# The second feed-forward matrix as a seven-product block scheme, interleaved with tiles of the first

## The reference, cut to what matters

```
f = rms_norm(h, g_ffn_pre)                    # [256, 2048]
f = square(relu(f @ w_ff1)) @ w_ff2           # w_ff1 [2048, 8192], w_ff2 [8192, 2048]
h = h + rms_norm(f, g_ffn_post)
```

## Time and profile before

| | |
|---|---|
| median of 3 runs | 2152.32 us (2152.02 to 2153.08) |
| span of the profiled execution | 2150.6 us |
| PE busy | 2125.1 us (99%) |
| DVE busy | 1361.9 us (63%) |
| ACT busy | 1106.1 us (51%) |
| POOL busy | 156.2 us (7%) |
| DMA, mean | 184 GB/s |
| PE clock granted, mean | 0.999 |

### The profile page before, as it was taken

The page is one execution under the profiler, slowest core; times in us unless marked ns, Lnnn a source line. Parts: engine busy times, 40 slices in busy tenths (PEclk is TensorE's granted clock), DMA queues, the critical chain, the costliest instruction groups (busy, mean ns, idle before and its releaser), DMA issues. The chain is left out here.

```text
span 2150.6 us, 29240 instructions
## 1 busy us (share of the span) xinstructions
PE 2125.1 (99%) x11602; PEld 1841.8 (86%) x11602; DVE 1361.9 (63%) x1979; ACT 1106.1 (51%) x1541; POOL 156.2 (7%) x78
## 2 busy tenths in 40 slices
PE   8999999999999999999999999999999999999998
PEld 7888888888988888888888888888888888888886
DVE  5554568875577558876578678766555555555555
ACT  4444554454464555555455455656435534544543
POOL 0000000000000000000007873000000000000000
PEclk9999999999999999999999999999999999999999
DMA  8666545655576655655656654646666666666664
GB/s 278 196 189 187 165 138 174 179 172 186 185 214 186 178 148 159 174 167 176 191 180 198 193 178 151 215 136 206 193 193 190 189 193 193 189 194 190 192 190 145
DMA packets 325031, 395.17 MB, mean 184 GB/s; under 512 B 20848, under 2 KB 252912, under 8 KB 324128
## 3 DMA queue, kind: packets, MB, share of 16 engines
q1 hardware_dynamic: 323104, 383.21, 59.0%
q0 software_dynamic: 1792, 10.10, 1.2%
HBM read 391.16 MB, written 2.10 MB: 183 GB/s over the span
## 5 line engine op out<-in xcount | busy, mean ns | idle before, releaser
L490 DVE TENSOR_TENSOR low<-raw,high 128x1024 fp32r<-128x1024 f32 (+2 forms) x672 | 809.9, 1209 | 639.0 <-ACT high L934 635.3
L934 ACT ACTIVATE high<-raw 128x1024 fp32r<-128x1024 f32 (+2 forms) x732 | 763.0, 1046 | 775.8 <-PE acc L682 201.7
L682 PE MATMUL acc<-xhl,high 128*128 128x512 f32 x3198 | 766.4, 391 | 0.0
L682 PEld LDWEIGHTS acc<-xhl,high 128*128 128x128 f32 x3198 | 587.0, 188 | 113.8 <-issue 0.7
L699 PE MATMUL acc<-xhl,low 128*128 128x256 f32 x3200 | 436.9, 286 | 1.9 <-DVE xhl L1792 1.4
L699 PEld LDWEIGHTS acc<-xhl,low 128*128 128x128 f32 x3200 | 414.4, 191 | 18.1 <-DVE xhl L1792 1.8
L686 PE MATMUL acc<-high,yhl 128*128 128x512 f32 (+1 forms) x1036 | 380.1, 373 | 2.2 <-DVE work L1718 1.6
L687 PE MATMUL acc<-high,yhl 128*128 128x512 f32 (+1 forms) x1036 | 378.8, 372 | 0.0
L702 PE MATMUL acc<-low,yhl 128*128 128x512 f32 (+1 forms) x1036 | 241.9, 374 | 0.2
L686 PEld LDWEIGHTS acc<-high,yhl 128*128 128x128 f32 x1036 | 195.2, 188 | 36.8 <-DVE work L1718 2.0
L687 PEld LDWEIGHTS acc<-high,yhl 128*128 128x128 f32 x1036 | 195.2, 188 | 33.8
(11 more groups left out here) (228 smaller groups left out, 1286.9 us busy)
## 6 DMA issues: line engine op xcount, KB each, us to landing
raw<-in_w_in SPq DMA_DIRECT2D x328, 512.0 KB, 3.7
raw<-in_w_ff SPq DMA_DIRECT2D x256, 512.0 KB, 3.9
raw<-in_w_out SPq DMA_DIRECT2D x91, 512.0 KB, 4.3
raw<-in_w_mem_kv SPq DMA_DIRECT2D x32, 512.0 KB, 5.0
raw<-in_w_in SPq DMA_DIRECT2D x16, 256.0 KB, 2.7
raw<-in_w_out SPq DMA_DIRECT2D x10, 256.0 KB, 2.8
x_nat<-in_mem SPq DMA_DIRECT2D x4, 512.0 KB, 7.8
x_nat<-in_x POOLq DMA_DIRECT2D x4, 512.0 KB, 6.4
```

The lines of the kernel that those rows point to most:

```text
L490: eng.tensor_tensor(part(low, g), part(raw, g), part(high, g).bitcast(F32), ALU.subtract).then_inc(ready, 1)
L682: ins = pe.matmul(acc[:, 2 * (c.acc % 2) + s, :], wh[:, t, at], vhl, start=first, stop=last)
L934: act.activation(part(high, g), part(raw, g), ACT.Copy).then_inc(high_ready, 1)
```

## The change

In mathematics: for the first 28 of 32 pairs of 128-row hidden tiles, and for half of the columns in the last 4 pairs, the 2x2 block product (two halves of the 256 rows, a pair of 128-row tiles, two halves of 1024 columns) is computed with seven block products in place of eight. A *group* is one such product: 256 hidden rows by 1024 columns of `w_ff2`, 60 groups in all. What is left of the matrix (4 pairs, columns 1024 to 2047) is done in 8 blocks as before (`last_block`).

- PE alternates: `group(g)`, 21 matmuls of 512 columns (seven products, for each the terms high-high, low-high, high-low one behind the other, each product in its own PSUM bank), and `hidden_tile(g+6)`, one tile of 128 hidden columns (16 matmuls of 512 columns, 16 of 256). The seven banks are emptied every fourth group.
- SP loads a group as two 512 KB transfers into one of two buffers (`load_group`), once PE has used the group two before.
- POOL forms the sums of the weight blocks (`group_sums`: two subtractions of 512 elements per partition, one of 1024), the sums of the hidden blocks (`pair_sums`: four of 128 elements, every second group) and the last additions (`add_sums`: two of 1024 elements, every fourth group).
- ACT rounds the seven weight units in three parts (`split_h`), the seven hidden units (`pair_h`), and copies a tile out of PSUM.
- DVE takes the low parts (`split_l`: 1024, 1024 and 1536 elements; `pair_l`: 896 every second group), folds and squares a hidden tile (`hidden_rows`: two of 256), takes the low parts of the two blocks of `w_ff1` (L518, in place in `raw`), and empties the banks (`sums_out`: seven of 512 every fourth group).

The core of the diff:

```diff
+PRODUCTS = ((2, 2, 1), (3, 3, 6), (1, 0, 0), (5, 1, 3), (6, 4, 4), (7, 5, 5), (4, 6, 2))
 PE
+            def group(g):
+                pe.wait_ge(pair_ready, pair + 1)
+                hid, units = hidden(pair), bset_r[:, g % 2]
+                for n, (p, unit, combo_no) in enumerate(PRODUCTS):
+                    pe.wait_ge(split_high, 3 * g + (1, 1, 2, 2, 3, 3, 3)[n])
+                    if first:
+                        product_released(g // 4, p)
+                    for hl in range(2):
+                        pe.matmul(bank_of[p], hid[:, hl, combo_no, :], units[:, 7 + unit, :], start=first and hl == 0,
+                                  stop=False)
+                    pe.wait_ge(split_low, 3 * g + (1, 1, 2, 2, 3, 3, 3)[n])
+                    ins = pe.matmul(bank_of[p], hid[:, 0, combo_no, :], units[:, unit, :], start=False, stop=last)
+                ins.then_inc(group_used, 1)
+            for g in range(GROUPS):
+                group(g)
+                if g + TILES_AHEAD < TILES:
+                    hidden_tile(g + TILES_AHEAD)
+            for i in range(4):
+                last_block(2, i, (0, 1))
 ACT
+            for g in range(GROUPS):
+                n, ahead = g + TILES_AHEAD - 1, g + 1 < GROUPS
+                if g and n < TILES:
+                    tile_copy(n)
+                if ahead:
+                    split_h(g + 1, 0)
+                    split_h(g + 1, 1)
...
+                round_block(FF1 + 2 * g + 2)
...
+                if ahead:
+                    split_h(g + 1, 2)
+                if g % 2 == 0 and n < TILES:
+                    pair_h(g // 2 + 2)
+                round_block(FF1 + 2 * g + 3)
 DVE
+            def split_l(g, part_no):
+                dve.wait_ge(sum_step, 3 * g + 3)
+                dve.wait_ge(split_high, 3 * g + part_no + 1)
+                at, end = ((2, 4), (0, 2), (4, 7))[part_no]
+                dve.tensor_tensor(bset_r[:, g % 2, at:end, :], bset[:, g % 2, at:end, :], bset_r[:, g % 2, 7 + at:7 + end, :].bitcast(F32),
+                                  ALU.subtract).then_inc(split_low, 1)
+            for g in range(GROUPS):
...
+                if g and n < TILES:
+                    hidden_rows(n)
+                if g:
+                    low_block(FF1 + 2 * g)
+                    low_block(FF1 + 2 * g + 1)
+                if ahead:
+                    split_l(g + 1, 0)
+                    split_l(g + 1, 1)
+                if g % 4 == 3:
+                    sums_out(g // 4)
+                if ahead:
+                    split_l(g + 1, 2)
+                if g % 2 == 0 and n < TILES:
+                    pair_l(g // 2 + 2)
 SP
+            def load_group(g):
+                if g < 2:
+                    sp.wait_ge(xt_ready, 40)
+                else:
+                    sp.wait_ge(group_used, g - 1)
...
 POOL
+            def group_sums(g):
+                units = bset[:, g % 2]
+                pool.wait_ge(group_landed[g % 2][0], 16 * (g // 2 + 1))
+                pool.tensor_tensor(units[:, 1, :], units[:, 1, :], units[:, 0, :], ALU.subtract).then_inc(sum_step, 1)
...
+            for g in range(GROUPS):
+                if g + 1 < GROUPS:
+                    group_sums(g + 1)
+                if g % 2 == 0 and g + TILES_AHEAD - 1 < TILES:
+                    pair_sums(g // 2 + 2)
+                if g % 4 == 0 and g:
+                    add_sums(g // 4 - 1)
```

More of the change, by code:

```diff
@@ L653, in weight_block @@
                 wh, wl = part(high, g), part(low, g)
-                tiles = [(t, c.kt0 + c.nk * i + t, s) for t in range(c.nk) for s in rows[:len(outs)]]
+                tiles = [(t, c.kt0 + c.nk * i + t, s) for t in range(c.nk) for s in range(2)]
                 crossed = k == ("f1", 0, 0) and i == 0
@@ new lines, in product_released @@
+            def product_released(k, p):
+                if k == 0:
+                    if p in (5, 6, 7, 4):
+                        pe.wait_ge(relu_ready, 2 if p in (5, 6) else 3)
+                elif p == 1:
+                    pe.wait_ge(first_out, k)
+                else:
+                    pe.wait_ge(out_step, 7 * (k - 1) + OUT_STEP[p])
+            def group(g):
+                pair, _ = where(g)
+                first, last = pair % 4 == 0, pair % 4 == 3
+                pe.wait_ge(pair_ready, pair + 1)
[10 more added lines that the diff above has]
+                ins.then_inc(group_used, 1)
@@ L914, in _ @@
                 transpose_unit(("h2T", u), x, 256 * u)
[L915 removed]
+            for b in range(12):
                 for u in {1: (2, 3), 3: (4, 5), 5: (6, 7)}.get(b, ()):
@@ L1248, in ff_side @@
[L1248 to L1267, removed]
@@ new lines, in first_copy @@
+            def first_copy(k):
+                act.wait_ge(group_used, 4 * k + 4)
+                if k:
+                    act.wait_ge(out_added, 2 * k - 1)
+                act.activation(au[:, 0, :], bank_of[1], ACT.Copy).then_inc(first_out, 1)
+            cross_out(("f1", 0, 0))
+            round_block(FF0 + 10)
+            round_block(FF0 + 11)
+            cross_out(("f1", 0, 1))
+            pair_h(0)
+            round_block(FF1)
+            for part_no in range(3):
+                split_h(0, part_no)
@@ new lines, in gain_sums @@
+            def gain_sums(n, n_sq):
+                dve.wait_ge(sq_ready, n_sq)
+                g = rowf[:, CW * n:CW * n + CW].unsqueeze(1).broadcast_to([P, ST, CW])
+                link(dve.tensor_tensor(m_cols(n), m_cols(n), g, ALU.mult))
+            fold(("f1", 0, 0))
+            first_tiles(0)
+            low_block(FF0 + 10)
+            low_block(FF0 + 11)
+            fold(("f1", 0, 1))
+            pair_l(0)
+            first_tiles(1)
+            low_block(FF1)
+            for part_no in range(3):
+                split_l(0, part_no)
@@ L1834, in _ @@
+            dve.wait_ge(sum_ready, sums("f2", 2))
+            gain_sums(2, n_sq + 6)
+            for s in range(ST):
+                rows, at = m_cols(3)[:, s, :], slice(s, s + 1)
                 if s:
-                    acc_done(last)
+                    dve.wait_ge(block_used, BLOCKS)
                 else:
                     dve.wait_ge(rows_half, 1)
-                dve.scalar_tensor_tensor(out=rows, in0=accs(last)[:, s, :], scalar=sq3[:, at], in1=rows, op0=ALU.mult,
-                                         op1=ALU.add).then_inc(sum_ready, 1)
@@ new lines, in _ @@
+            group_sums(0)
+            pair_sums(0)
+            pair_sums(1)
+            for g in range(GROUPS):
+                if g + 1 < GROUPS:
[4 more added lines that the diff above has]
+                    add_sums(g // 4 - 1)
+                if g == GROUPS - 2:
+                    pool.wait_ge(block_used, LAST0)
+                    pool.dma_start(rowf, a["g_ffn_post_2"][0].partition_broadcast(P)).then_inc(rowf_landed, 16)
```

390 lines of the change are left out of this document (296 added, 94 removed).

## The result

The changed kernel takes 2345.76 us (median of 4 runs, 2344.59 to 2346.58), the kernel before 2152.70 beside it: 1.0896 times as long, 95% interval 1.0880 to 1.0911. The forecast was 2317 us, with a range of 2195 to 2400. The profiled span is 2342.8 us.

What follows compares the result with a forecast made beforehand. PE bounds the kernel before; after the change DVE and POOL in turns do. 33.4 + 13 + 58 x 13.8 (800.4) + 21.8 = 868.6 against 703.7, 165 us more: 2317 us, range 2195 to 2400.

Steps and rivals of the forecast that it cites:

- PE's pace: Per round of one group and one tile, PE needs 21 x 0.227 + 5.56 = 10.32 us.
- Who sets the pace: In the 58 rounds, DVE with POOL taking turns exceeds PE's 10.32 us, so PE waits.
- The round: One group and one tile: 7.50 + 6.76 - 0.8 = 13.4 us to 14.6; 13.8 taken.
- the proportion taken from the row: POOL's short sums: 0.10 us plus a proportional part of 2.36, giving 1.23 for 512 elements, 0.38 for 128.
- two thirds of `sums_out`: In the round, two thirds of DVE's bank emptying (1.13 us a round) was taken to run beside POOL's work: 13.8 us.
- the turns' gain: In the round, 0.15 us back for each POOL instruction DVE stands behind, 5.5 per round, at most 0.8 us.
- The bounds: Limits for the round of DVE and POOL: between 12.6 and 15.0 us, giving 2248 to 2387 us.
- Where PE waits: In each group, PE waits for `split_l` at the last matmuls, the high-low term.
- the worse rival: In the rounds, PE's pauses lower its clock and DVE waits for the tile: round of 16, 2445 us; 11%.
- most rounds: Sign of a wrong forecast: the granted clock falls below 1 in most of the 58 rounds.
- the first hidden units: At the part's start, PE waits some 2 us for these and sums; the start's terms together are 13 us.
- The same chain with one addition in another form, taken as nothing: Behind the last matmul, the remaining work was claimed unchanged but for one addition's form, adding nothing.

Runs made afterwards that it cites:

- the runs with fills: Against the changed kernel, POOL's nine kinds of sums became fills that read nothing, short or of twice the elements; sums left out of the result: 2134.80 and 2135.00 us.
- all on DVE: Against the changed kernel, all of POOL's sums moved to DVE, nothing left out: 2250.33 us, 1.0456 of the kernel before.
- the run with short fills: Against the changed kernel, POOL's nine kinds of sums became fills of the same elements, sums left out of the result: 2134.80 us, 0.9918 of the kernel before.
- the added fills: Against the changed kernel, POOL got four extra scratch fills of 512 two-byte elements in each of 55 rounds: 2356.88 us, ratio 1.0949 to the kernel before.

## Why the prediction was right, step by step

- PE's pace. 10.32 us a round was worked out; where nothing else holds it, it is 10.32 or 10.33 (the runs with fills; 10.31 with their last round, which is shorter).
- Who sets the pace. DVE with POOL, as forecast: 99% busy with no wait of its own, its instructions long. Taking POOL's reads away removes the loss, with POOL half busy writing too; adding reads adds 123 us, and adding writes 11.
- The round: 13.8 forecast, 13.86 measured. Of its parts, 512 elements on POOL took 1.27 alone (1.23 taken), 128 elements 0.46 (0.38 taken), and DVE's list of 8.63 + 3.6 for the sums gives 12.2, where 12.30 was measured with all on DVE. The page "GPSIMD Engine Reference" of the Trainium skill, section "Performance versus the Vector engine", weighed there at 1.1 us for 512 elements, was further off than the proportion taken from the row. By its 2.6 cycles the 2816 elements of a round's POOL work are an estimated 6.1 us, 0.7 less than 6.76 and not 0.3, as the prediction has it.
- What in the 13.8 was luck. With the lengths measured alone POOL's work of a round is 7.0 us, not 6.76; so 15.6 us of work took 13.86, and 1.8 us overlapped where 1.6 were counted. The two errors cancel. That two thirds of `sums_out` run beside POOL was a guess, and no run separates it from the turns' gain. The bounds were also added wrongly: by their own terms they are 12.8 and 15.4 us a round, not 12.6 and 15.0, and so about 2259 and 2410 us, the upper one just outside the stated range. None of this touches the direction.
- That the turn is taken whole, and only between reads, was the row's reading and that of the Trainium skill, "SBUF — State Buffer", section "Who interferes with whom": the fills, which that page exempts, cost nothing measurable with POOL up to 273 of 550 us busy.
- Where PE waits: in part wrong. I had put it at the group's last matmuls. It waited 82.6 us in the tile for the low part of `w_ff1` and 22.6 for the split. With PE off the path this cost the forecast nothing.
- The clock. The ingredient of the worse rival came true; in the rounds its price did not. The granted clock fell to 0.92 there on average, and below 1 in 26 of the 58 rounds, just short of the "most rounds" named as a sign of being wrong; in 5 us windows it reads down to 0.50, the lower of the two levels. This is also why PE is busy 83% and not near 75%. PE had the time: DVE waited 4.3 us in all for a tile's copy, and the granted clock returned to 1.00 when POOL's reads went. At the start and the end of the part, where PE is waited for, the price was paid (below).
- DVE's instructions. Close to 100% busy was right; "many near 2.4 to 3.5" was too much, since the median low block is at 1.22.
- The forecast is 29 us short by the medians and 27 by the profiled span. Of these 27, 14 lie at the start, 3 in the rounds (58 x 0.06) and 10 at the end. The start: by the forecast's terms group 1 begins at 1479.9 (2315.6 of span, less 800.4 for the rounds and 35.3 behind group 59), and it began at 1493.9. In the rows of the changed kernel PE had done five of the seven products and then sat idle 7.31 us:

```profile
1476.53 0.40 PE L839 MATMUL acc<-bset_r,hid 128*128 128x512 f32 x1
1484.24 1.19 PE L836 MATMUL acc<-bset_r,hid 128*128 128x512 f32 x2 [7.31 <-DVE combo L2006]
```

The sixth product's bank is freed by the third tile of `w_ff1` (`relu_ready`), which on DVE stands behind the first split, the row sums and `pair_l(1)`. I had looked only at the first hidden units. The same wait is 6.62 us in the run with short fills, so it does not come from POOL's reads. Before it PE had waited 1.83 us for a low part. These are 9.1 of the 14 us; the other 4.9 are PE at the lower clock after each pause, here (us, PE busy, clock, DMA share, GB/s) and at the end of the part:

```profile
1485.00:1490.00 5.00, 5.00 (x14) 0.51 0.35 93
...
2295.00:2300.00 5.00, 2.25 (x5) 0.55 0.59 210
```

The end: from group 59 to the end of the span I had 35.3 us (4.76 for the group, 21.8, and 8.7 behind the last matmul) and it is 45.0, in the run with short fills 45.1. Group 59 comes after a pause of 6.86 us and takes 2.2 us more at the lower clock; 1.1 go by until its first bank is emptied; the last eight blocks take 2.8 more; and behind the last matmul there are 12.3 us, 3.6 more. DVE's last rows in the changed kernel show the last two:

```profile
2322.06 1.22 DVE L518 TENSOR_TENSOR raw_r<-raw,high 128x1024 fp32r<-128x1024 f32 x1
2323.33 1.22 DVE L2067 TENSOR_TENSOR msum<-msum,rowf 128x1024 f32<-128x1024 f32 x1
...
2327.49 1.22 DVE L2067 TENSOR_TENSOR msum<-msum,rowf 128x1024 f32<-128x1024 f32 x1 [1.61 <-ACT tail L1200]
2328.74 0.69 DVE L2123 TENSOR_TENSOR msum<-msum,tb 128x512 f32<-128x512 f32 x1
...
2334.28 0.68 DVE L2123 TENSOR_TENSOR msum<-msum,tb 128x512 f32<-128x512 f32 x1
```

PE waited 2.05 us for the last low block (2322.06), which stands behind a gain that waits for ACT's squares of the first columns; and the chain of the first half of the rows (L2123 at 2328.74) starts behind a gain that waits for ACT, so that the chain of the second half (2334.28) follows the first instead of PE's last matmul, which ends at 2330.5. "The same chain with one addition in another form, taken as nothing" is the term that was mis-sized: it measured 3.6 us, and not for the form of the addition but for its place. A second term left out was the lower clock at both ends, about 7 us together.

## What to carry to other kernels

Before arithmetic is moved to GpSimd to relieve VectorE, look at what VectorE runs beside it: if both of its inputs are in SBUF and GpSimd reads SBUF, add the two times (here 8.6 and 7.0 us took 13.9); the sum, not the larger, must fit under the engine that sets the pace. In such a place the cheaper engine per element should do all of it, even if it is the fuller one, and GpSimd costs next to nothing only for fills or beside instructions with an input in PSUM. Added work on GpSimd can also cost by coming late, as the added fills show. A scheme that saves matmuls pays in elementwise work, so count that first: here PE could gain 40.8 us in all, while the sums ask 3.7 us of DVE in each of 58 rounds, or 5.2 with POOL in turns, and a round at PE's pace leaves DVE 1.7.

## What the runs showed of the hardware that was not expected

- Both engines lose by taking turns, and the shorter instruction loses most: 128 elements on POOL take 0.46 us alone and 1.32 to 1.44 beside DVE. A queue of short instructions advances by one for each long one of the other.
- A POOL read costs the kernel less than its length, 0.56 us for 0.75 alone; of these 0.24 are longer DVE instructions and 0.31 DVE's waits, chiefly for the work queued behind it on POOL.
- PE's granted clock reads 0.51 and 0.55 in the 5 us windows in which PE works again after pauses of 7.31 and 6.86 us. This costs where PE is waited for (start and end of the part) and hardly anything in rounds that DVE sets.
- A POOL fill of 2-byte elements takes as long per element as one of 4-byte elements: 1024 in 0.951 us and in 0.956.
